# Norms with root and reciprocal on full rows in place of four columns

## The chip, the cores and the metric

The kernel runs on one core of one Trainium2 chip. Its engines are TensorE (PE, matmuls), VectorE (DVE), ScalarE (ACT), GpSimd (POOL) and SyncE (SP, which issues most of the loads). The metric is the device time of one execution in microseconds.

## The reference

Two blocks, one behind the other, on x of 512 positions by 1024 features, all in float32. The first block has four layers (Hyena, window attention, pooling, Hyena), each a mixer and a feed-forward part. The second has one layer (gated delta rule beside latent attention, a merge, and an MLP) with a modulation. Ahead of each of these ten parts stands a norm over the 1024 features:

```python
def rmsnorm(x, g):
    xf = x.astype(jnp.float32)
    y = xf * lax.rsqrt(jnp.mean(xf * xf, axis=-1, keepdims=True) + EPS)
    return (y * g.astype(jnp.float32)).astype(x.dtype)
...
    for i in range(DEPTH):
        h = rmsnorm(x, norm_mix[i])
        ...
        x = x + y
        x = x + swiglu(rmsnorm(x, norm_ffn[i]), ff_w_gate[i], ff_w_up[i], ff_w_down[i])
...
        h = _modulate(_rms(x, norm_attn[l]), mod_x[0], mod_x[1])
        ...
        x = x + mod_x[5] * _sq_relu_mlp(_modulate(_rms(x, norm_mlp[l]), mod_x[3], mod_x[4]), w_mlp_in[l], w_mlp_out[l])
```

## The kernel before

x lies in SBUF as eight tiles of 128 features by 512 positions (`x[:, k, :]`, k from 0 to 7), features on the partitions. A norm sums over features, so over the partitions, and that sum is made by a matmul with ones. `xn` is the buffer for the squares and then for the normed x.

Each engine has its own program, written out by hand stage by stage in the order of `schedule_of`, and the engines wait for each other on semaphores only. Weights come in blocks of 1 MB through a ring of four (`ring`). For the feed-forward parts, the Hyena projections and the MLP each weight and each x is split into a high part of reduced width and the rest: ACT writes the high part (`w_hi`, line 1765; `z_lo` and others, line 1777; of x `x_hi`, line 1772), POOL subtracts it from the weights (`w_lo`, line 779; `ring_r`, line 803), DVE subtracts it from x (`low`, line 2334, into `x_lo` or, in the Hyena layers, `xn_r`). PE then makes three matmuls per tile (lines 904 to 906 for the first block of a stage, 893 to 895 behind it) as soon as the tile's rest is there.

A norm works like this. ACT squares each tile of x when the residual is added (line 1781); DVE adds seven of them into `xn[:, 0]` (`fold`, line 2365). PE multiplies each quarter of 128 positions of that sum, used as the weights, with one column of ones (line 873), then the same for the eighth square (line 877). So the sum for position 128c + p stands on partition p in column c, four columns in all. DVE adds the two groups (lines 2375, 2376), ACT takes the root (line 1810; line 1806 is a root of one number that loads the table of functions early), DVE the reciprocal (line 2380). PE turns the four columns back into a full tile, the same row on all 128 partitions, with the identity (line 882), and DVE multiplies each of the eight tiles of x by the gain and by this tile, which it reads from PSUM (line 2355, in the modulated norms line 2668 with 2669). `rows_read` (line 2386) is a small memset whose semaphore frees the PSUM bank. The banks for such side results are four, taken in turn by a count (`aux`) that every engine keeps in step.

Attention norms its heads with a root and a reciprocal on whole tiles of 128x512 (lines 1105, 1967, 2555, 2557).

Of the kernel before, what the change touches and what calls it, by code (L numbers as in the profile page):

```python
# [268 lines left out]
def run(handlers, schedule):  # L269

    for name, arg in schedule:
        handlers[name](arg)
# [7 lines left out]
def build_program(nc, stream, vecs, tabs, tabs2, x_in, ctx_in, first_mods, scratch, x_keep, diag, solved_t, solved_n, out, schedule):  # L280
# [4 lines left out]
    with ExitStack() as stack:  # L285
# [3 lines left out]
        def sem(name):  # L289
            return stack.enter_context(nc.semaphore(name))  # L290
# [57 lines left out]
        one_col = small_t[:, 7:8]  # L348
        rstd_col = small_t[:, 28:32]

# [17 lines left out]
        def V(name, j=0, n=1, rows=P):  # L368
            at, _ = VEC[name]
            return vec[0:rows, at + j:at + j + n]  # L370
# [25 lines left out]
        folded_set = sem("folded_set")  # L396
        rstd_set = sem("rstd_set")
        root_set = sem("root_set")
# [159 lines left out]
        def _(sp):  # L558
# [43 lines left out]
            def norm(_):  # L602
                n["aux"] += 2
                n["xn"] += DT
# [34 lines left out]
            def modulate(which):  # L639
                n["aux"] += 2 if which else 3  # L640

# [77 lines left out]
        def _(pool):  # L719
# [101 lines left out]
            def passes(aux, acc):  # L821
                def stage(_):
# [4 lines left out]
            nothing = count(0)  # L827
            run({"norm": count(2), "hyena": hyena,
                 "attention": passes(12 + 16 * 5, 88), "pool": passes(0, DT), "ffn": split("ffn", FT + 2 * DT), "mod": nothing,
                 "modulate": lambda which: n.update(aux=n["aux"] + (2 if which else 3)), "decays": count(2),  # L830
                 "gdn": gdn, "mla": nothing, "merge": merge,
# [4 lines left out]
        def _(pe):  # L836
# [31 lines left out]
            def norm(gain):  # L868
                b = open_aux()
                n["fold"] += 1  # L870
                pe.wait_ge(folded_set, n["fold"])
                for c in range(NB):
                    mm(b[:, c:c + 1], xn[:, 0, P * c:P * (c + 1)], ones[:, 0:1], start=True, stop=True)
                n["sq"] += DT
                pe.wait_ge(squares_set, n["sq"])
                for c in range(NB):
                    ins = mm(b[:, NB + c:NB + c + 1], xn[:, DT - 1, P * c:P * (c + 1)], ones[:, 0:1], start=True, stop=True)
                ins.then_inc(aux_full, 1)
                b = open_aux()
                pe.wait_ge(rstd_set, n["fold"])  # L880
                for c in range(NB):
                    ins = mm(b[:, P * c:P * (c + 1)], rstd_col[:, c:c + 1].broadcast_to([P, P]), ident[:], start=True, stop=True)
                ins.then_inc(aux_full, 1)
                n["xn"] += DT
# [842 lines left out]
        def _(act):  # L1727
# [61 lines left out]
            def norm(gain, then=None):  # L1789
# [16 lines left out]
                step(go(small_t[:, 26:27], one_col, ACT.Sqrt))  # L1806
                t = aux.take()
                aux.take()
                act.wait_ge(aux_drained[aux.place(t)], aux.turn(t) + 1)
                signal(go(rstd_col, rstd_col, ACT.Sqrt, bias=eps_col, scale=1.0 / D), root_set)  # L1810
                if split_target(gain) == "hyena":
# [489 lines left out]
        def _(dve):  # L2301
# [40 lines left out]
            def norm(gain):  # L2342
# [3 lines left out]
                if gain == ("norm_mix", 2 * DT):  # L2346
                    nc.vector.memset(sums[:], 0.0)
                    signal(nc.vector.memset(xp[:], 0.0), pads_set)
                    signal(tt_(bs_col, V("pl_b", 0, DT), V("pl_scale", 0, DT), ALU.mult), pads_set)
                t, rows = rstd_rows()  # L2350
                n["xn"] += DT
                target = split_target(gain)
                to = (x_hi_h, xn_r) if target == "hyena" else (x_hi, x_lo)
                for k in range(DT):
                    signal(stt(xn[:, k, :], x[:, k, :], V(gain[0], gain[1] + k), rows, ALU.mult, ALU.mult),  # L2355
                           plain_set if target else xn_set)
                    if target and k:
                        low(k - 1, *to)
                rows_read(t)
                if target:  # L2360
                    low(DT - 1, *to)

            def fold(k):
# [4 lines left out]
                else:  # L2368
                    signal(ins, folded_set)
                    n["sq"] += DT  # L2370

            def rstd_rows():
                t = full(aux, aux_full)
                b = bank(t, True)
                step(nc.vector.tensor_copy(rstd_col, b[:, 0:NB]))
                ins = tt_(rstd_col, b[:, NB:2 * NB], rstd_col, ALU.add)
                drain(ins, t, True)
                n["root"] += 1
                dve.wait_ge(root_set, n["root"])
                signal(nc.vector.reciprocal(rstd_col, rstd_col), rstd_set)  # L2380
                t = full(aux, aux_full)
                return t, bank(t, True)[:]

            def rows_read(t):
                which = aux_drained[t % BANKS]
                nc.vector.memset(small_t[:, 25:26], 0.0).then_inc(which, 1)
                dve.wait_ge(which, t // BANKS + 1)

# [270 lines left out]
            def modulate(which):  # L2659
# [3 lines left out]
                for c in range(2 - which):  # L2663
                    step(ts_(gm[:, c, :], modv[:, scale:scale + DT, c], 1.0, None, ALU.add))
                    step(tt_(gm[:, c, :], gm[:, c, :], gain, ALU.mult))
                t, rows = rstd_rows()
                for k in range(DT):
                    step(stt(xn[:, k, :], x[:, k, :], gm[:, 0, k:k + 1], rows, ALU.mult, ALU.mult))
                    signal(ts_(xn[:, k, :], xn[:, k, :], modv[:, shift + k, 0:1], None, ALU.add), plain_set if which else xn_set)
                    if which and k:  # L2670
                        low(k - 1)
                rows_read(t)
                if which:
# [665 lines left out]
```

## Time and profile before

| | |
|---|---|
| median of 3 timed runs | 4458.51 us (4454.24 to 4459.21) |
| profiled execution | 4452.26 us, span 4450.5 us |
| mean granted clock of PE | 0.956 |
| busy, share of the span | PE 94%, PE weight loads 70%, DVE 47%, POOL 32%, ACT 28% |

The span runs from the first to the last instruction. The granted clock is the share of 2.4 GHz that PE was allowed; its two levels are 2.4 GHz (1.00) and 1.2 GHz (0.50). A matmul in full float32 shows as two records. Where a row of the timeline has a bracket, it gives the engine's idle time before the instruction and what ended it.

### The profile page before, as it was taken

What the parts mean: (1) busy time and instruction counts of PE and PEld (TensorE: products, weight loads), DVE (VectorE), ACT (ScalarE), POOL (GpSimd) and SP (SyncE); (2) the same over time, 40 slices, a digit from 0 to 9 for tenths busy, and PEclk for the clock granted to TensorE, in tenths of its full rate; (3) what the DMA queues carried; (4) which work ended last, traced back from release to release, by engine and by line L of the source; (5) the groups of instructions that cost most, each with busy time, mean ns of one, the idle gap of its engine ahead of it and who ended that gap; (6) DMA issues with size and microseconds to landing.
All of it is one profiled execution on the core that took longest, in us unless ns stands there. A gap on an engine that the chain in (4) does not pass through costs nothing.

```text
span 4450.5 us, 48055 instructions
## 1 busy us (share of the span) xinstructions
PE 4174.7 (94%) x19126; PEld 3110.0 (70%) x19126; DVE 2094.2 (47%) x3123; ACT 1229.7 (28%) x1725; POOL 1442.8 (32%) x834
## 2 busy tenths in 40 slices
PE   7999999999999699999999999989999899998999
PEld 6656788656788478877557887556666665685887
DVE  6567333365323641365773334456664357403322
ACT  3322222135222221233232122322322224422221
POOL 3311344200344144433123442256564000231343
PEclk9999999999999899999999998989999879999999
DMA  6200222210232123221003221121211121221232
GB/s 181 76 15 20 110 108 86 101 55 20 107 107 84 68 101 111 83 81 62 34 29 121 91 104 59 55 59 31 58 33 57 58 76 58 76 95 62 90 104 76
DMA packets 96910, 333.73 MB, mean 75 GB/s; under 512 B 44336, under 2 KB 47536, under 8 KB 67888
## 3 DMA queue, kind: packets, MB, share of 16 engines
q1 hardware_dynamic: 87968, 311.85, 19.8%
q10 hardware_dynamic: 8720, 18.82, 1.7%
q8 instruction: 152, 2.49, 0.2%
q14 instruction: 70, 0.57, 0.0%
HBM read 317.53 MB, written 13.11 MB: 74 GB/s over the span
## 4 chain that ended last, share of the span: by engine, by line
PE 81%; DVE 13%; ACT 2%; POOL 2%; issue 2%; DMA 0%; SPq 0%; DVEq 0%; ACTq 0%; POOLq 0%
PE bank L893 16%; PE bank L894 16%; PE bank L895 16%; PE bank L1328 5%; PE bank L864 5%; PE bank L1095 2%; PE bank L1045 2%; PE bank L1069 1%; PE bank L1308 1%; PE bank L1629 1%; PE bank L1628 1%; PE bank L1650 1%; PE bank L1560 1%; DVE xn L2355 1%; PE bank L1589 1%
## 5 line engine op out<-in xcount | busy, mean ns | idle before, releaser
L779 POOL TENSOR_TENSOR w_lo<-ring,w_hi 128x2048 fp32r<-128x2048 f32 (+2 forms) x200 | 775.1, 3876 | 1519.6 <-ACT w_hi L1765 1519.6
L893 PE MATMUL bank<-x_hi,w_hi 128*128 128x512 f32 x1584 | 618.3, 390 | 9.0 <-POOL w_lo L779 9.0
L895 PE MATMUL bank<-x_hi,w_lo 128*128 128x512 f32 x1584 | 616.9, 389 | 0.0
L894 PE MATMUL bank<-x_lo,w_hi 128*128 128x512 f32 x1584 | 616.7, 389 | 0.0
L1765 ACT ACTIVATE w_hi<-ring 128x2048 fp32r<-128x2048 f32 (+2 forms) x200 | 322.0, 1610 | 867.0 <-PE bank L895 866.0
L893 PE MATMUL bank<-h_hi,w_hi 128*128 128x512 f32 x960 | 373.9, 389 | 0.4
L894 PE MATMUL bank<-h_lo,w_hi 128*128 128x512 f32 x960 | 373.5, 389 | 0.0
L895 PE MATMUL bank<-h_hi,w_lo 128*128 128x512 f32 x960 | 373.4, 389 | 0.0
L893 PEld LDWEIGHTS bank<-x_hi,w_hi 128*128 128x128 f32 x1584 | 297.7, 188 | 72.5 <-POOL w_lo L779 11.1
L895 PEld LDWEIGHTS bank<-x_hi,w_lo 128*128 128x128 f32 x1584 | 297.6, 188 | 62.1
L894 PEld LDWEIGHTS bank<-x_lo,w_hi 128*128 128x128 f32 x1584 | 297.7, 188 | 61.6
L2409 DVE TENSOR_TENSOR xn<-bank,xn 128x512 f32<-128x512 f32 x88 | 60.8, 691 | 587.0 <-PE bank L895 567.6
L1328 PE MATMUL bank<-xn,ring 128*128 128x512 f32 x496 | 237.5, 617 | 1.4 <-DVE work L2712 1.4
L1095 PE MATMUL bank<-work,tab 128*128 128x512 f32 x512 | 225.7, 598 | 12.7 <-ACT work L1908 11.7
L2399 DVE TENSOR_TENSOR x<-bank,x 128x512 f32<-128x512 f32 x72 | 49.8, 691 | 394.1 <-PE bank L895 347.7
L792 POOL TENSOR_TENSOR ring_r<-ring,merge_hi 128x2048 fp32r<-128x2048 f32 x16 | 73.3, 4584 | 499.1 <-ACT merge_hi L2240 499.1
L893 PEld LDWEIGHTS bank<-h_hi,w_hi 128*128 128x128 f32 x960 | 180.2, 188 | 39.5 <-DVE h_lo L2340 2.1
L894 PEld LDWEIGHTS bank<-h_lo,w_hi 128*128 128x128 f32 x960 | 180.2, 188 | 37.3
L895 PEld LDWEIGHTS bank<-h_hi,w_lo 128*128 128x128 f32 x960 | 180.2, 188 | 37.3
L1095 PEld LDWEIGHTS bank<-work,tab 128*128 128x128 f32 x512 | 97.2, 192 | 131.7 <-issue 125.6
L815 POOL TENSOR_TENSOR work<-work,ring 128x1024 f32<-128x1024 f32 x32 | 76.8, 2426 | 265.1 <-ACT work L1877 265.1
L766 POOL TENSOR_TENSOR tab<-tab 56x31 f32<-56x31 f32 (+15 forms) x248 | 152.4, 615 | 19.4
(461 smaller groups left out, 7435.3 us busy)
## 6 DMA issues: line engine op xcount, KB each, us to landing
ring<-stream SPq DMA_DIRECT2D x212, 1024.0 KB, 4.8
ring<-stream SPq DMA_DIRECT2D x64, 704.0 KB, 4.0
ring<-stream SPq DMA_DIRECT2D x36, 512.0 KB, 3.5
xn<-first_mods SPq DMA_DIRECT2D x8, 1024.0 KB, 7.0
ring<-stream SPq DMA_DIRECT2D x4, 1088.0 KB, 5.1
bias_rows<-work ACTq DMA_DIRECT2D x1, 4096.0 KB, 46.2
work<-bias_rows ACTq DMA_DIRECT2D x1, 3072.0 KB, 12.0
tab<-tabs ACTq DMA_DIRECT2D x1, 2624.0 KB, 16.8
```

The source lines that it names most:

```text
L766: solve(tt(W[:, 0:i, i:SUB], W[:, 0:i, i:SUB], part, ALU.subtract))
L779: nc.gpsimd.tensor_tensor(w_lo[:, j % 2, 0:cols], ring[:, k % RING, 0:cols], w_hi[:, j % 2, 0:cols], ALU.subtract).then_inc(wlo_set, 1)
L792: nc.gpsimd.tensor_tensor(ring_r[:, w, 0:2 * DT * P], ring[:, w, 0:2 * DT * P], merge_whi[j % 2][:], ALU.subtract).then_inc(wlo_set, 1)
L815: nc.gpsimd.tensor_tensor(pair, pair, decay[:, pq:pq + 1, :].broadcast_to([P, 2, 512]), ALU.mult).then_inc(filt_set, 1)
L864: ins = mm(b[:], w[:, at + k, :], rhs[k] if isinstance(rhs, list) else rhs[:, k, :], start=(k == 0), stop=(k == kt - 1))
L893: mm(b[:], hi[:, at + k, :], rhs_hi, start=(k == 0), stop=False)
L894: mm(b[:], hi[:, at + k, :], rhs_lo[:, k, :], start=False, stop=False)
L895: ins = mm(b[:], lo[:, at + k, :], rhs_hi, start=False, stop=(k == kt - 1))
L1045: ins = mm(b[:, 256 * p:256 * (p + 1)], U[:, 4 * ft + 2 * kind + p, ct * P:(ct + 1) * P], inv[kind][:, p, ft, :], start=(j == 0), stop=(j ...
L1095: ins = mm(b[:], fwd[kind][:, p, q, ft * P:(ft + 1) * P], source(kind)[:, 2 * p + q, :], start=(q == 0), stop=(q == 1))
L1328: ins = mm(b[:, 0:TC] if ctx else b[:], w[:, at + k, :], src[:, k, :], start=(k == 0), stop=(k == DT - 1))
L1765: signal(go(w_hi[:, j % 2, 0:cols], ring[:, k % RING, 0:cols], ACT.Copy), whi_set)
```

## The change

In all ten norms the sums are made as full rows: two matmuls with the whole matrix of ones as weights and the squares as the moving side, added up in one bank. Every partition then holds the sum of every position. ACT takes the root of this 128x512 tile into SBUF (`rstd`), DVE the reciprocal of 128x512 in place, which also frees the bank, and the multiplications read `rstd` from SBUF instead of a bank. The four columns, the two small DVE operations, PE's second visit and the closing memset are gone, and each norm takes one side bank instead of two. The norm of the context, the pool layer and the order of stages are untouched.

```diff
             def norm(gain):            # PE
                 b = open_aux()
                 n["fold"] += 1
                 pe.wait_ge(folded_set, n["fold"])
-                for c in range(NB):
-                    mm(b[:, c:c + 1], xn[:, 0, P * c:P * (c + 1)], ones[:, 0:1], start=True, stop=True)
+                mm(b[:], ones[:], xn[:, 0, :], start=True, stop=False)
                 n["sq"] += DT
                 pe.wait_ge(squares_set, n["sq"])
-                for c in range(NB):
-                    ins = mm(b[:, NB + c:NB + c + 1], xn[:, DT - 1, P * c:P * (c + 1)], ones[:, 0:1], start=True, stop=True)
-                ins.then_inc(aux_full, 1)
-                b = open_aux()
-                pe.wait_ge(rstd_set, n["fold"])
-                for c in range(NB):
-                    ins = mm(b[:, P * c:P * (c + 1)], rstd_col[:, c:c + 1].broadcast_to([P, P]), ident[:], start=True, stop=True)
-                ins.then_inc(aux_full, 1)
+                mm(b[:], ones[:], xn[:, DT - 1, :], start=False, stop=True).then_inc(aux_full, 1)
                 n["xn"] += DT
...
                 step(go(small_t[:, 26:27], one_col, ACT.Sqrt))      # ACT
-                t = aux.take()
-                aux.take()
-                act.wait_ge(aux_drained[aux.place(t)], aux.turn(t) + 1)
-                signal(go(rstd_col, rstd_col, ACT.Sqrt, bias=eps_col, scale=1.0 / D), root_set)
+                t = full(aux, aux_full)
+                signal(go(rstd, bank(t, aux=True)[:], ACT.Sqrt, bias=eps_col, scale=1.0 / D), root_set)
...
-                t, rows = rstd_rows()                               # DVE
+                t = aux.take()
+                n["root"] += 1
+                dve.wait_ge(root_set, n["root"])
+                drain(nc.vector.reciprocal(rstd, rstd), t, True)
...
                 for k in range(DT):
-                    signal(stt(xn[:, k, :], x[:, k, :], V(gain[0], gain[1] + k), rows, ALU.mult, ALU.mult),
+                    signal(stt(xn[:, k, :], x[:, k, :], V(gain[0], gain[1] + k), rstd, ALU.mult, ALU.mult),
                            plain_set if target else xn_set)
                     if target and k:
                         low(k - 1, *to)
-                rows_read(t)
...
-            def rstd_rows():
-                t = full(aux, aux_full)
-                b = bank(t, True)
-                step(nc.vector.tensor_copy(rstd_col, b[:, 0:NB]))
-                ins = tt_(rstd_col, b[:, NB:2 * NB], rstd_col, ALU.add)
-                drain(ins, t, True)
-                n["root"] += 1
-                dve.wait_ge(root_set, n["root"])
-                signal(nc.vector.reciprocal(rstd_col, rstd_col), rstd_set)
-                t = full(aux, aux_full)
-                return t, bank(t, True)[:]
```

`modulate` on DVE changes in the same way as `norm`.

What stands on VectorE from the last addition of squares in the first norm, before (`bank` is PSUM, `vec` the gains, `small_t` holds the four columns):

```order
L2365 TENSOR_TENSOR xn<-xn 128x512 [waits squares_set,vec_step] x5
L2375 COPY small_t<-bank 128x4 [waits aux_full,folded_set]
L2376 TENSOR_TENSOR small_t<-bank,small_t 128x4 [waits vec_step]
L2380 RECIPROCAL small_t<-small_t 128x4 [waits root_set,aux_drained0]
L2355 SCALAR_TENSOR_TENSOR xn<-x,vec,bank 128x512 [waits aux_full,rstd_set]
L2355 SCALAR_TENSOR_TENSOR xn<-x,vec,bank 128x512 [waits plain_set]
L2334 TENSOR_TENSOR xn_r<-xn,x_hi_h 128x512 [waits xhi_set,plain_set]
```

and at the same place of the changed kernel (its line numbers are its own; `rstd_t` holds `rstd`):

```order
L2355 TENSOR_TENSOR xn<-xn 128x512 [waits squares_set,vec_step] x5
L2341 RECIPROCAL rstd_t<-rstd_t 128x512 [waits root_set,folded_set]
L2346 SCALAR_TENSOR_TENSOR xn<-x,vec,rstd_t 128x512 [waits aux_drained0]
L2346 SCALAR_TENSOR_TENSOR xn<-x,vec,rstd_t 128x512 [waits plain_set]
L2322 TENSOR_TENSOR xn_r<-xn,x_hi_h 128x512 [waits xhi_set,plain_set]
```

The copy and the addition are gone, the reciprocal has full rows, and the multiplications have three SBUF operands and no wait for PE.

On TensorE the same place before, with the first matmuls of the Hyena layer behind it:

```order
L873 MATMUL bank<-ones,xn 128x1 [waits folded_set,consts_set]
L873 MATMUL bank<-ones,xn 128x1 x3
L877 MATMUL bank<-ones,xn 128x1 [waits squares_set]
L877 MATMUL bank<-ones,xn 128x1 x3
L882 MATMUL bank<-ident,small_t 128x128 [waits rstd_set]
L882 MATMUL bank<-ident,small_t 128x128 x3
L1720 MATMUL bank<-tab,vec 16x512 [waits tab_landed,vec_landed]
L952 MATMUL bank<-tab,vec 64x512
L904 MATMUL bank<-x_hi_h,z_lo 128x512 [waits xn_set,wlo_set]
```

and in the changed kernel:

```order
L870 MATMUL bank<-xn,ones 128x512 [waits folded_set,consts_set]
L873 MATMUL bank<-xn,ones 128x512 [waits squares_set]
L1710 MATMUL bank<-tab,vec 16x512 [waits tab_landed,vec_landed]
L942 MATMUL bank<-tab,vec 64x512
L894 MATMUL bank<-x_hi_h,z_lo 128x512 [waits xn_set,wlo_set]
```

Twelve small matmuls have become two long ones, and PE's wait for the reciprocal in the middle is gone; it waits for the normed x alone.

## Rows read from the trace of the kernel before

**Rows 1.** The page: chain that ended last, shares of the span by engine

```profile
PE 81%; DVE 13%; ACT 2%; POOL 2%; issue 2%; DMA 0%; SPq 0%; DVEq 0%; ACTq 0%; POOLq 0%
```

**Rows 2.** Timeline at 471.7: start us, us, engine line op [idle before]

```profile
471.05 0.69 DVE L2365 TENSOR_TENSOR xn<-xn 128x512 f32<-128x512 f32 x1
...
471.89 1.02 PE L873 MATMUL bank<-ones,xn 128*128 128x1 f32 x8 [1.73 <-DVE xn L2365]
...
477.25 1.53 DVE L2355 SCALAR_TENSOR_TENSOR xn<-x,vec,bank 128x512 f32<-128x512 f32 x2 [2.30 <-PE bank L882]
...
479.66 0.76 PE L904 MATMUL bank<-x_hi,w_hi 128*128 128x512 f32 x1 [2.52 <-DVE x_lo L2334]
```

**Rows 3.** Lines of DVE, 400 to 4450: busy us, mean ns | idle before

```profile
L2355 DVE SCALAR_TENSOR_TENSOR xn<-x,vec,bank 128x512 f32<-128x512 f32 x56 | 41.9, 748 | 17.6 <-PE bank L882 15.9
...
L2668 DVE SCALAR_TENSOR_TENSOR xn<-x,gm,bank 128x512 f32<-128x512 f32 x16 | 12.0, 747 | 5.1 <-PE bank L882 4.6
...
L2380 DVE RECIPROCAL small_t<-small_t 128x4 f32<-128x4 f32 x9 | 1.6, 178 | 4.7 <-ACT small_t L1810 4.7
...
L2375 DVE COPY small_t<-bank 128x4 f32<-128x4 f32 x9 | 1.5, 161 | 18.4 <-PE bank L877 18.4
...
L2376 DVE TENSOR_TENSOR small_t<-bank,small_t 128x4 f32<-128x4 f32 x9 | 1.5, 161 | 0.3
...
L2347 DVE MEMSET work<- 128x1056 f32 x1 | 0.9, 938 | 0.3 <-DVE xn L2365 0.3
...
L2665 DVE TENSOR_TENSOR gm<-gm,vec 128x8 f32<-128x8 f32 x3 | 0.5, 168 | 0.1
```

**Rows 4.** Timeline of one root and reciprocal in attention

```profile
872.32 1.02 PE L1105 MATMUL bank<-work,tab 128*128 128x512 f32 x2
...
873.44 0.69 ACT L1967 ACTIVATE work<-bank,small_t 128x512 f32<-128x512 f32 x1 [0.26 <-PE bank L1105]
...
874.23 3.35 DVE L2555 RECIPROCAL work<-work 128x512 f32<-128x512 f32 x1 [17.41 <-ACT work L1967]
...
877.69 0.75 DVE L2557 SCALAR_TENSOR_TENSOR work<-bank,vec,work 128x512 f32<-128x512 f32 x1
```

**Rows 5.** Timeline: matmuls at half clock, in three norms

```profile
15.91 1.84 PE L873 MATMUL bank<-ones,xn 128*128 128x1 f32 x8 [15.91 <-DVE xn L2365]
...
22.64 1.89 PE L1720 MATMUL bank<-tab,vec 33*16 33x512 f32 x2
...
1932.08 1.83 PE L873 MATMUL bank<-ones,xn 128*128 128x1 f32 x8 [2.02 <-DVE xn L2365]
...
2750.90 1.54 PE L877 MATMUL bank<-ones,xn 128*128 128x1 f32 x8
```

**Rows 6.** Timeline: DVE beside POOL in the first norm and behind it

```profile
22.33 4.51 POOL L803 TENSOR_TENSOR ring_r<-ring,z_lo 128x2048 fp32r<-128x2048 f32 x1 [20.71 <-ACT z_lo L1777]
...
22.82 1.53 DVE L2355 SCALAR_TENSOR_TENSOR xn<-x,vec,bank 128x512 f32<-128x512 f32 x2 [2.23 <-PE bank L882]
...
24.39 2.99 DVE L2334 TENSOR_TENSOR xn_r<-xn,x_hi_h 128x512 fp32r<-128x512 f32 x1
...
41.31 4.49 POOL L803 TENSOR_TENSOR ring_r<-ring,z_lo 128x2048 fp32r<-128x2048 f32 x1 [14.48 <-ACT z_lo L1777]
...
42.15 3.94 DVE L2432 TENSOR_SCALAR work<-work 64x512 f32<-64x512 f32 x1 [4.60 <-ACT work L1854]
...
62.07 0.75 DVE L2451 SCALAR_TENSOR_TENSOR work<-work,vec 128x512 f32<-128x512 f32 x1
...
62.44 4.86 POOL L803 TENSOR_TENSOR ring_r<-ring,z_lo 128x2048 fp32r<-128x2048 f32 x1 [4.47 <-ACT z_lo L1777]
...
62.86 5.00 DVE L2452 SCALAR_TENSOR_TENSOR work<-work,vec 128x512 f32<-128x512 f32 x1
```

**Rows 7.** Stretch (us, five engines' busy, granted clock); timeline at 1558

```profile
477.00:484.00 7.00, 4.48 (x11) 3.46 (x11) 6.47 (x9) 3.12 (x5) 0.00 (x0) 0.50 0.01 2
...
1558.45 4.50 POOL L779 TENSOR_TENSOR w_lo<-ring,w_hi 128x2048 fp32r<-128x2048 f32 x1 [69.80 <-ACT w_hi L1765]
```

More of the change, by code:

```diff
@@ L348, in build_program @@
         one_col = small_t[:, 7:8]
-        rstd_col = small_t[:, 28:32]
         def carve(*sizes):
@@ L396, in build_program @@
         folded_set = sem("folded_set")
-        rstd_set = sem("rstd_set")
         root_set = sem("root_set")
@@ L602, in norm @@
             def norm(_):
-                n["aux"] += 2
+                n["aux"] += 1
                 n["xn"] += DT
@@ L639, in modulate @@
             def modulate(which):
-                n["aux"] += 2 if which else 3
+                n["aux"] += 1 if which else 2
             def decays(_):
@@ L827, in _ @@
             nothing = count(0)
-            run({"norm": count(2), "hyena": hyena,
+            run({"norm": count(1), "hyena": hyena,
                  "attention": passes(12 + 16 * 5, 88), "pool": passes(0, DT), "ffn": split("ffn", FT + 2 * DT), "mod": nothing,
-                 "modulate": lambda which: n.update(aux=n["aux"] + (2 if which else 3)), "decays": count(2),
+                 "modulate": lambda which: n.update(aux=n["aux"] + (1 if which else 2)), "decays": count(2),
                  "gdn": gdn, "mla": nothing, "merge": merge,
@@ L2370, in fold @@
                     n["sq"] += DT
-            def rstd_rows():
-                t = full(aux, aux_full)
-                b = bank(t, True)
-                step(nc.vector.tensor_copy(rstd_col, b[:, 0:NB]))
-                ins = tt_(rstd_col, b[:, NB:2 * NB], rstd_col, ALU.add)
-                drain(ins, t, True)
-                n["root"] += 1
-                dve.wait_ge(root_set, n["root"])
-                signal(nc.vector.reciprocal(rstd_col, rstd_col), rstd_set)
-                t = full(aux, aux_full)
-                return t, bank(t, True)[:]
[L2384 to L2387, printed above, removed]
             def residual(bias_name=None, scale_name=None, fold_squares=True):
@@ L2665, in modulate @@
                     step(tt_(gm[:, c, :], gm[:, c, :], gain, ALU.mult))
-                t, rows = rstd_rows()
+                t = aux.take()
+                n["root"] += 1
+                dve.wait_ge(root_set, n["root"])
+                drain(nc.vector.reciprocal(rstd, rstd), t, True)
                 for k in range(DT):
-                    step(stt(xn[:, k, :], x[:, k, :], gm[:, 0, k:k + 1], rows, ALU.mult, ALU.mult))
+                    step(stt(xn[:, k, :], x[:, k, :], gm[:, 0, k:k + 1], rstd, ALU.mult, ALU.mult))
                     signal(ts_(xn[:, k, :], xn[:, k, :], modv[:, shift + k, 0:1], None, ALU.add), plain_set if which else xn_set)
@@ L2671, in modulate @@
                         low(k - 1)
-                rows_read(t)
                 if which:
```

## The prediction

> **What bounds the kernel now.** I read the chain that ended last first: it is 81% on TensorE (PE) [rows 1]. So only time in which PE waits, or in which something that it waits for is late, can change the end. Then I read the timeline around the norms. A norm is a place where everything waits for one chain. In [rows 2] the last partial sum of squares on VectorE (DVE) ends at 471.74 (471.05 + 0.69). PE then makes eight small matmuls (16 records), DVE and ScalarE (ACT) work on four columns, PE spreads them over the rows again, and the first multiplication of x starts at 477.25. This chain from the fold to the first multiplication took 5.51 us. PE's first real product starts at 479.66, 2.41 us behind the multiplication. PE has no other work in that time, so the length of this chain is paid in full, once per norm. There are ten such norms.
>
> DVE's groups of lines give the same chain for the nine norms behind the first [rows 3]: idle before L2375 18.4, its busy 1.5; L2376 1.5 and 0.3; idle before L2380 4.7, its busy 1.6; waits for PE before L2355 and L2668 15.9 and 4.6. That is 48.5 us. In the pool layer's norm two memsets stand in this chain (2 x 0.94 and 0.5 of idle time), and in the two norms with modulation small work on the gains adds 1.2 (L2665 0.5 and 0.1, L2664 the same). Together 52.1 us, or 5.8 per norm.
>
> **What replaces it.** Per norm: two matmuls 128x512 with a matrix of ones, a square root 128x512 on ACT straight from PSUM, a reciprocal 128x512 on DVE, and the same eight multiplications, now with the factor from SBUF. Attention of this very kernel has the same three steps in the same shapes [rows 4], so nothing has to be guessed but what surrounds them:
> - fold to PE: 0.15 (471.74 to 471.89, [rows 2]);
> - two matmuls. One is two records, which take 1.02 together and 0.59 alone, so 0.43 lies between starts [rows 4]. Four records: 1.02 + 2 x 0.43 = 1.88;
> - PE to ACT 0.10, root 0.69, ACT to DVE 0.10 [rows 4];
> - reciprocal 3.35, then 0.11 until the next instruction [rows 4].
>
> The sum is 6.38 us. The reciprocal on four columns took 0.18 [rows 3]: the price of the change is that this one instruction becomes 3.2 us longer, and what it buys is the second visit to PE (2.30 of wait in [rows 2]), the two small DVE operations and the shorter sum on four columns. Nine norms: 9 x 6.38 = 57.4 against 52.1, **+5.3 us**. The two memsets of the pool norm are hidden in this sum, because DVE now waits for ACT anyway.
>
> The eight multiplications keep their price: 748 ns with the factor from PSUM [rows 3], and 0.75 for the same instruction with all tensors in SBUF (L2451 at 62.07 [rows 6]). The memset of L2386 that frees the bank goes. At 59 ns it stood mostly under a rounding on ACT; only in the pool norm is DVE itself the pace, -0.14 with its gap.
>
> **TensorE's clock in the sums.** PE has had no work for 1.73 us when the sums begin (the idle time in the row of L873, [rows 2]), and the granted clock falls from 2.4 to 1.2 GHz somewhere in the gap. In the norm of 1932 the half clock had come before the sums: the same eight records took 1.83 instead of 1.02 [rows 5, 2]. The new sums are longer, so more of them meet it. At half clock two records of 512 columns take 1.89 (L1720 [rows 5]), so four take 1.89 + 2 x 0.86 = 3.61, that is +1.73 over 1.88. If the clock falls where it fell before: +1.73 in the norm of 1932; about +1.0 in the norm of 2750, where the second group of eight records took 1.54 [rows 5]; and, as my estimate, +0.5 each in the norms near 845 and 1500, where it fell later. Bounds: nothing, and 9 x 1.73 = 15.6. I take the same places: **+3.7 us**. After the chain PE restarts at half clock now as before (0.50 granted from 477 to 484, [rows 7]); the phase of that is left out as even on the mean, with about 1 us either way per norm and some 2 us over all.
>
> **VectorE and GpSimd.** In the first norm GpSimd (POOL) subtracts the high part of the weights from 22.33 to 26.84 while DVE multiplies [rows 6]. The two multiplications with a PSUM factor ran through it undisturbed (1.53 for two). The first subtraction with two SBUF tiles, L2334, did not: it took 2.99 instead of 0.69 and ended at 27.38, 0.54 after POOL. The multiplication form that will be used now, all from SBUF, shows the same: L2452 at 62.86 took 5.00 and ended 0.56 after POOL's subtraction that ended at 67.30 [rows 6]. So in the first norm: the sums start at 15.91 at half clock (the small group took 1.84, [rows 5]) and end at 15.91 + 3.61 = 19.5, about where the small ones do; root and reciprocal end at 23.8; then the first multiplication is held until 27.40. The second takes 0.78 with its gap, the subtraction 0.7: it ends at 28.9 instead of 27.38, **+1.5 us**. If the multiplication were not held, it would be 0. This delay is passed on: the last tile releases ACT's rounding, behind that stands the rounding of the next weights, and for that POOL waited 14.48 us at 41.31 [rows 6], with PE behind it. In the norm of 1556 POOL works from 1558.45 to 1562.95 [rows 7]; by my sum the reciprocal ends at 1562.8, so the first multiplication meets only its last 0.1 us. In the other eight norms POOL has ended its work before DVE multiplies, or starts after it.
>
> The reciprocal itself reads one SBUF tile. The trace has no long reciprocal beside POOL. The nearest row is L2432, a one-tile operation that was held from 42.15 until 0.29 after POOL's end [rows 6]; another one-tile row is L2355, which was not held. Held, the reciprocal at 1559.4 would end near 1566.2 (+3.4), and the one at 20.4, if it held POOL in its turn until 23.8, would move POOL's end by 1.5. I take it as not held: it takes 3.35 us for 512 elements where a multiplication takes 0.75 [rows 4], so it is the slowest reader of its tile of them all and has no use for a second way into SBUF, and in this it is nearer to L2355 than to the quick L2432, whose 64x512 would be done in well under a us. The Trainium skill says this as a rule (SBUF — State Buffer, Who interferes with whom): a VectorE instruction with at most one SBUF input that is outside the 2-port modes does not contend with GpSimd, one with two SBUF inputs contends with a GpSimd instruction that reads SBUF. By it the first price is 0 and the multiplication's is 1.5; for the reciprocal no row here shows it.
>
> **Sum.** +5.3 + 3.7 - 0.1 + 1.5 = **+10.4 us**. The profiled execution took 4452.26 us (span 4450.5), the median of the timed runs is 4458.51, 6.25 above it; I carry that difference over: 4458.5 + 10.4 = 4468.9, say 4469, 0.23% more. A measurement of this kernel tells about 0.2% (8.9 us) from no change, so the forecast stands just over that bound.
>
> **Rivals.**
> - *The clock spares the sums.* If the full clock holds for the 1.9 us of sums in all nine norms, 3.7 falls away: +6.7, 4465. And the norm of 1932 is cheaper than before. For it: in [rows 2] the group ran at full clock, 1.02. Against: the new sums are longer, and the row of 1932 had lost the clock before they began. Chance 0.2.
> - *The reciprocal is caught by POOL.* +10.4 + 3.4 + 1.5 = +15.3, 4474. For it L2432's row, against it the rate. Chance 0.1.
> - *Not slower: the dense sums keep PE's clock up.* Before, the 16 records in the gap were 128x1 and did little; now PE multiplies 1.9 us in full. If the clock then stayed at 2.4 GHz until the restart, the 3.7 would go, and in the four norms in which PE itself sets the pace behind the restart (471, 845, 1127 and 2377) so would the half-clock stretch, (484 - 479.7) / 2 = 2.2 each at least [rows 2, 7], 8.6 in all. 10.4 - 3.7 - 8.6 = -1.9, 4457. It decides from the point where at least five of these things happen. Against it: PE stands still for 4.4 us behind the sums and another 2.4 until the first product, longer in one piece than the gap in the middle of the chain before, in which the clock was low. The Trainium skill gives a rule that bears on this (TensorE: Matmul & The Clock Gate, Why this matters for your kernels): avoid idle gaps between bursts of matmuls, or the clock goes back to half. By this rule the rival doesn't come about, and the trace agrees as far as it goes: half clock from 477 to 484 behind a gap of this length [rows 7]. Chance 0.06.
> - *The steps overlap more than I think*, with a result within 5 us of before: nothing in the timeline stands beside the chain that could do it. Chance 0.04.
>
> **How the numbers follow.** The forecast has 0.6, with its own range of +7.5 to +13.5 (what share of the clock's 15.6 is met, and the restart). Within it some 0.45 of 0.6 lie above 8.9 us. Slower: 0.45 + 0.1 = 0.55. Within 0.2%: 0.15 + 0.2 + 0.05 + 0.03 = 0.42 with rounding. Faster: 0.03. The range for 8 of 10 reaches from the first rival's lower side to the second rival with some us of a run's own spread: 4461 to 4477.
>
> **What would show it.** Right: ten reciprocals of 128x512 at 3.35 us; about 6.4 us from fold to first multiplication where the clock is full and up to 8.1 where it isn't; no L882; in the first norm a multiplication of over 3 us that ends 0.56 after POOL; PE's busy time lower, which buys nothing. Wrong: multiplications of 0.75 beside POOL; PE records of 0.39 right after the gap; a reciprocal of over 3.4 us; a chain under 6 us anywhere.

## The result and the profile after

The changed kernel takes 4472.98 us (median of 7 runs, 4467.73 to 4479.67), the kernel before 4458.51 in the same comparison (7 runs, 4453.41 to 4461.94): ratio 1.0032, 95% interval 1.002 to 1.0044, so 14.5 us slower. The profiled execution took 4467.73, the shortest of the seven (span 4465.9, before 4450.5: +15.4).

The page after, busy time by engine, the granted clock in its 40 slices, and the chain that ended last:

```profile
PE 4158.9 (93%) x18926; PEld 3081.6 (69%) x18926; DVE 2120.0 (47%) x3093; ACT 1233.6 (28%) x1725; POOL 1442.7 (32%) x834
...
PEclk9999999999999899999989999989998879999999
...
PE 81%; DVE 13%; ACT 2%; POOL 2%; issue 1%; DMA 0%; SPq 0%; DVEq 0%; ACTq 0%; POOLq 0%
```

The page tells little: 200 PE records fewer, 26 us more on DVE, and shares of the chain as before [rows 1]. The timeline after, of the norm of [rows 2]:

```profile
466.62 0.69 DVE L2355 TENSOR_TENSOR xn<-xn 128x512 f32<-128x512 f32 x1
...
467.46 1.10 PE L870 MATMUL bank<-xn,ones 128*128 128x512 f32 x2 [1.73 <-DVE xn L2355]
468.39 1.02 PE L873 MATMUL bank<-xn,ones 128*128 128x512 f32 x2
...
469.51 0.69 ACT L1798 ACTIVATE rstd_t<-bank,small_t 128x512 f32<-128x512 f32 x1 [0.69 <-PE bank L873]
470.30 3.35 DVE L2341 RECIPROCAL rstd_t<-rstd_t 128x512 f32<-128x512 f32 x1 [2.99 <-ACT rstd_t L1798]
473.69 1.54 DVE L2346 SCALAR_TENSOR_TENSOR xn<-x,vec,rstd_t 128x512 f32<-128x512 f32 x2
```

From the fold's end (467.31) to the first multiplication it is 6.38 us. It is 6.38 in eight of the nine later norms, the modulated ones too, and 6.67 in the one near 2386. The groups of lines after, DVE and PE from 400 to 4450 (busy us, mean ns | idle before), stand where [rows 3] stood:

```profile
L2346 DVE SCALAR_TENSOR_TENSOR xn<-x,vec,rstd_t 128x512 f32<-128x512 f32 x56 | 42.1, 752 | 2.0
...
L2341 DVE RECIPROCAL rstd_t<-rstd_t 128x512 f32<-128x512 f32 x7 | 23.5, 3354 | 18.7 <-ACT rstd_t L1798 18.7
...
L2642 DVE RECIPROCAL rstd_t<-rstd_t 128x512 f32<-128x512 f32 x2 | 6.7, 3353 | 4.8 <-ACT rstd_t L1798 4.8
```

```profile
L870 PE MATMUL bank<-xn,ones 128*128 128x512 f32 x18 | 9.9, 630 | 15.3 <-DVE xn L2355 15.3
L873 PE MATMUL bank<-xn,ones 128*128 128x512 f32 x18 | 9.2, 592 | 0.0
```

The sums ran at 2.4 GHz in all nine norms: each of the 18 records of L873 took 592 or 593 ns, and of L870 the first of each norm took 667 and the second 592 (at half clock, in the first norm, they took 1061 and more). The 6.67 near 2386 does not come from PE: there the sums ended at 2388.59 and ACT began its root at 2388.97, 0.38 behind them, where it is 0.10 in the norm above; why is open. The timeline after, of the first norm:

```profile
20.52 3.35 DVE L2341 RECIPROCAL rstd_t<-rstd_t 128x512 f32<-128x512 f32 x1 [4.78 <-ACT rstd_t L1798]
...
22.44 4.50 POOL L801 TENSOR_TENSOR ring_r<-ring,z_lo 128x2048 fp32r<-128x2048 f32 x1 [20.82 <-ACT z_lo L1767]
23.91 4.36 DVE L2346 SCALAR_TENSOR_TENSOR xn<-x,vec,rstd_t 128x512 f32<-128x512 f32 x2
...
28.31 0.69 DVE L2322 TENSOR_TENSOR xn_r<-xn,x_hi_h 128x512 fp32r<-128x512 f32 x1
...
29.15 0.77 PE L894 MATMUL bank<-x_hi_h,z_lo 128*128 128x512 f32 x1 [7.16 <-DVE xn_r L2322]
```

The reciprocal kept its 3.35 with POOL beside it for the last 1.4 us. Near 1556 a whole reciprocal (from 1556.32) lay inside a subtraction of POOL (1555.34 to 1559.84) and took 3.35 too. Two multiplications took 4.36 in place of 1.53, and PE's first product came at 29.15, 1.6 later than before (27.53).

**Where the time went.** I cut both profiled executions at the end of each norm's fold (the last addition of squares) and at its last multiplication, and compare the pieces (us). A stage is what lies between a norm's last multiplication and the next fold's end.

| piece | before | after | difference |
|---|---|---|---|
| ten chains, fold to first multiplication | 59.3 | 65.9 | +6.6 |
| eight multiplications, ten times | 102.4 | 103.3 | +0.8 |
| first Hyena stage | 436.0 | 430.0 | -6.1 |
| second Hyena stage | 427.3 | 439.9 | +12.6 |
| delta-rule and latent stage | 1303.3 | 1306.1 | +2.8 |
| all other stages and the end | 2122.2 | 2120.9 | -1.3 |

The chains and multiplications give 7.4, half of what was measured. The other half lies in stages whose instructions were not changed. A half-clock stretch is from here on one in which PE was granted 1.2 GHz. In the Hyena stages one iteration of the loop over filters takes 61.5 us or 65.0 us. Two stretches of one iteration's length, us, five engines' busy time and the granted clock; before:

```profile
2155.00:2216.50 61.50, 56.08 (x194) 34.00 (x193) 40.84 (x52) 16.74 (x25) 9.30 (x4) 0.97 0.00 1
```

and after, then three pieces of such an iteration:

```profile
2155.00:2220.00 65.00, 59.56 (x194) 35.66 (x193) 40.98 (x52) 16.74 (x25) 9.34 (x4) 0.92 0.00 1
...
2222.00:2228.00 6.00, 6.00 (x16) 2.88 (x16) 5.76 (x9) 2.16 (x4) 0.00 (x0) 1.00 0.00 1
2228.70:2232.10 3.40, 3.40 (x28) 2.94 (x26) 1.29 (x2) 0.00 (x0) 0.00 (x0) 1.00 0.00 0
2232.20:2239.00 6.80, 6.80 (x14) 3.70 (x15) 0.18 (x1) 1.22 (x3) 0.97 (x1) 0.50 0.00 0
```

The same 194 matmul records, 3.5 us more of PE busy. Both iterations have one half-clock stretch of 3.4 us behind PE's wait for the spectra's product; the long one has a second, of 6.8 us. Ahead of that second stretch PE was busy without a gap, but with 28 records in 3.4 us: these are the filter-magnitude sums, sixteen matmuls against a single column of ones. The stretch begins at 2232.22, 2.9 us after the sums did and inside them. The lines on PE after (L1075 is the sums, L1059 the filter's taps behind them):

```profile
2222.48 7.03 PE L1085 MATMUL bank<-work,tab 128*128 128x512 f32 x16
2229.35 4.20 PE L1075 MATMUL bank<-ones,work 128*128 128x1 f32 x32
2233.41 9.91 PE L1059 MATMUL bank<-ring,work 128*128 128x512 f32 x16
```

Before, the same sixteen were followed by taps at full clock, 7.12 in place of 9.91:

```profile
2227.25 3.63 PE L1085 MATMUL bank<-ones,work 128*128 128x1 f32 x32
2230.74 7.12 PE L1069 MATMUL bank<-ring,work 128*128 128x512 f32 x16
```

In every profile of a kernel with these sums a stage that has had one long iteration has only long ones from there on. So a stage comes out at 427 to 431 with none and at 436 to 442 with one to four. That a small change of timing decides between the two was then my theory 1; theory 2 was that a delay costs its own length and the change has a further price of its own.

### The profile page after: what moved, and what is told of

Its sections match the earlier page's. It is cut to its first block, busy times and chain, and to the rows that moved or that the text cites. A ratio compares the mean times of both kernels' runs of the same rounds, so it can differ in the third digit from the quotient of the medians.

```text
span 4465.9 us, 47595 instructions
## 1 busy us (share of the span) xinstructions
PE 4158.9 (93%) x18926; PEld 3081.6 (69%) x18926; DVE 2120.0 (47%) x3093; ACT 1233.6 (28%) x1725; POOL 1442.7 (32%) x834
## 4 chain that ended last, share of the span: by engine, by line
PE 81%; DVE 13%; ACT 2%; POOL 2%; issue 1%; DMA 0%; SPq 0%; DVEq 0%; ACTq 0%; POOLq 0%
PE bank L883 16%; PE bank L884 16%; PE bank L885 16%; PE bank L1318 5%; PE bank L862 5%; PE bank L1085 2%; PE bank L1035 2%; PE bank L1059 1%; PE bank L1298 1%; PE bank L1619 1%; PE bank L1618 1%; PE bank L1640 1%; DVE xn L2346 1%; PE bank L1550 1%; PE bank L1579 1%
## 5 line engine op out<-in xcount | busy, mean ns | idle before, releaser
L1085 PE MATMUL bank<-work,tab 128*128 128x512 f32 x512 | 225.9, 599 | 12.8 <-ACT work L1896 11.7
```

What stands on the lines that cost most here:

```text
L1085: ins = mm(b[:], fwd[kind][:, p, q, ft * P:(ft + 1) * P], source(kind)[:, 2 * p + q, :], start=(q == 0), stop=(q == 1))
```

## Experiments

All ratios are to the kernel before, timed on the same chip in the same series; each series had another chip. In the first four series its median was 4456.4, 4455.3, 4455.7 and 4454.1 (4442.9 to 4465.3 over all); in the fifth, with a_wide64_again alone, it was 4464.0. Stage lengths are from each run's one profiled execution.

**b_head1**: a delay at the start alone, in the kernel before.

```diff
-                    for k in range(1, DT - 1):
+                    for k in range(1, DT - 2):
                         fold(k)
+                    step(nc.vector.memset(kbuf2[:, 0:772], 0.0))
+                    step(nc.vector.memset(kbuf2[:, 0:96], 0.0))
+                    fold(DT - 2)
```

> The kernel before with two memsets on DVE (772 and 96 columns, some 0.9 us together) ahead of the last partial sum of the first norm, nothing else changed. Everything behind it starts 0.9 us later. Theory 1 (the part of the slowdown that the norm chains don't explain comes from half-clock stretches in the Hyena and delta-rule stages, and their number depends on the moment at which a stage begins): the total moves by something else than 0.9 us, anywhere from -8 to +10 us, and the two Hyena stages (436.0 and 427.3 us in the profile before, from the first norm multiplication... to the next fold) change length by steps of about 1.7 us, the time that a half-clock stretch of 3.4 us costs. Theory 2 (a delay costs its own length, and the change has a further price of its own): +0.9 us, both stages as before within 1 us.

Measured: 4473.52 (10 runs, 4465.13 to 4480.36), ratio 1.0038 [1.0026, 1.0051]. A delay of 0.9 us costs 17. That is outside theory 1's own range (-8 to +10) as well as far from theory 2's 0.9. Both Hyena stages were long, 439.3 and 440.1. The timed runs say the same as the profile: five took 4465.1 to 4470.3 at a mean granted clock of 0.952 to 0.953, the other five 4476.8 to 4480.4 at 0.950, and the kernel before in the same series runs from 0.958 in its shortest run (4443.1) to 0.953 in its longest (4464.2).

**b_head2**: the two memsets twice, 1.8 us.

> As the run before it, with twice the memsets (some 1.8 us). Theory 1: the total moves by another amount than with 0.9 us and not by twice as much, with stage lengths in steps of 1.7 us. Theory 2: +1.8 us.

Measured: 4475.59 (6 runs), ratio 1.0045 [1.0028, 1.0061]; Hyena stages 431.0 and 441.3. The second 0.9 us costs 2.1, which is less than the spread of the six runs (4467.20 to 4481.19): not 17 again.

**b_slow**: the kernel before with the same two memsets ahead of the reciprocal in each of the ten norms.

```diff
+                for cols in (772, 96):
+                    step(nc.vector.memset(kbuf2[:, 0:cols], 0.0))
                 signal(nc.vector.reciprocal(rstd_col, rstd_col), rstd_set)
```

> The kernel before with the same two memsets (0.9 us) in each of the ten norm chains, ahead of the reciprocal on four columns, so that each chain is 0.9 us longer as in the changed kernel (0.87), with the sums, the PSUM factor and all else as before. Theory 1 (chain length and its shifts are all there is): +9 us of chains, and of the stretches anything from -8 to +10, so that the total can equal the changed kernel's +14.5. Theory 2 (the change has a further price beside its chains): +9 us and no more, both Hyena stages as before.

Measured: 4467.62 (12 runs), ratio 1.0025 [1.0014, 1.0036]. Its chains sum to 71.0, 11.7 more than before, and it costs 11.2: ten delays cost less than one at the head, and in its profiled execution (4463.39; the runs reach 4475.03) both Hyena stages were short (431.2, 429.9). So the excess does not grow with the delay. This run alone would also fit theory 2, which had +9.

**a_psum**: the changed kernel with the reciprocal written to the norm's PSUM bank and read from there.

```diff
-                drain(nc.vector.reciprocal(rstd, rstd), t, True)
+                rows = bank(t, True)[:]
+                step(nc.vector.reciprocal(rows, rstd))
...
-                    signal(stt(xn[:, k, :], x[:, k, :], V(gain[0], gain[1] + k), rstd, ALU.mult, ALU.mult),
+                    signal(stt(xn[:, k, :], x[:, k, :], V(gain[0], gain[1] + k), rows, ALU.mult, ALU.mult),
```

> The changed kernel, with the reciprocal written to its PSUM bank and the eight multiplications reading it there, and the closing memset back. If GpSimd's hold on the multiplication with SBUF operands cost 1.6 us in the first norm, then the first multiplication there takes 0.75 us and not 3.6, the first product of the matmul engine comes 1.5 us sooner than in the changed kernel (27.6 and not 29.15), and the other chains stay at 6.4 us. If the hold is not the cause, the first product stays at 29.1. The total: -1.5 us against the changed kernel, beside what the stretches do.

Measured: 4473.62 (8 runs), ratio 1.0033 [1.002, 1.0046], as the changed kernel. The first norm's timeline shows that its own purpose was reached:

```profile
22.40 4.51 POOL L801 TENSOR_TENSOR ring_r<-ring,z_lo 128x2048 fp32r<-128x2048 f32 x1 [20.78 <-ACT z_lo L1767]
23.88 1.53 DVE L2347 SCALAR_TENSOR_TENSOR xn<-x,vec,bank 128x512 f32<-128x512 f32 x2
...
25.45 2.01 DVE L2322 TENSOR_TENSOR xn_r<-xn,x_hi_h 128x512 fp32r<-128x512 f32 x1
...
27.61 0.77 PE L894 MATMUL bank<-x_hi_h,z_lo 128*128 128x512 f32 x1 [6.03 <-DVE xn_r L2322]
```

The multiplications run free again, the next operation with two SBUF operands (L2322, 2.01 for 0.69) is the one held, and PE starts at 27.61 instead of 29.15. The 1.5 us are real, and lost again: both Hyena stages were long (442.1, 440.1).

**b_wide64, a_wide64, b_wide128**: take away the suspected trigger. The filter-magnitude sums get 64 (128) columns of ones in place of one; the same edit in the kernel before (b) and the changed one (a).

```diff
-                        ins = mm(b[:, ct:ct + 1], mags[:, pq, ct * P:(ct + 1) * P], ones[:, 0:1],
+                        ins = mm(b[:, 64 * ct:64 * (ct + 1)], mags[:, pq, ct * P:(ct + 1) * P], ones[:, 0:64],
...
-                    drain(nc.vector.reciprocal(invn[:, 4 * c:4 * c + 4], bank(t, True)[:, 0:4]), t, True)
+                    drain(nc.vector.reciprocal(invn[:, 4 * c:4 * c + 4], bank(t, True)[:, 0:256:64]), t, True)
```

> The kernel before, with the sixteen N=1 matmuls of each filter-magnitude sum in the Hyena stages (L1085, moving operand 128x1) given a moving operand of 64 columns of ones instead; results and their readers are the same, so only the columns that TensorE streams change. Theory 1 (recurring half-clock stretches of the Hyena stages are the cause of the 8 us that the norm chains do not explain, and the 6.8 us stretch of each loop iteration is set off by these N=1 matmuls): the 6.8 us stretches are gone from both Hyena stages, each stage lasts 427 to 432 us in every run, and the kernel's times gather at 4443 to 4452, 5 to 10 below its median of 4456, with less spread than the 21 us of before. Theory 2 (the stages' length has another cause, and the clock only follows it): both lengths, 427 to 431 and 436 to 442, still occur, the times still spread over some 20 us, and the median moves by under 3 us. If the 64 columns cost time by themselves (at most 16 x 0.1 us in eight places), up to 13 us come on top.

> The changed kernel with the same edit (64 columns in place of one in the filter-magnitude matmuls of the Hyena stages). Theory 1: its Hyena stages also last 427 to 432 us, and its distance to the kernel before with the same edit is what the ten chains cost, 5.5 + 1.6 = +7 us, not +14.5: about 4450 to 4459. Theory 2: the distance between the two stays at 14 to 15 us.

> The kernel before with 128 columns in place of one in the same sixteen matmuls. Theory 1: as with 64 columns, no 6.8 us half-clock stretch, times within 4 us of those with 64 columns plus what 64 more columns cost (16 x 0.1 us in eight places at most, if the weight loads do not hide them: up to 13 us). Theory 2: no change of the spread.

Measured:

| kernel | median us, runs | lowest, highest | ratio [95%] | Hyena stages |
|---|---|---|---|---|
| b_wide64 | 4447.29, 11 | 4440.41, 4449.66 | 0.9977 [0.9968, 0.9986] | 428.7, 427.4 |
| a_wide64 | 4455.10, 11 | 4453.39, 4459.10 | 1.0 [0.9991, 1.0009] | 428.8, 425.5 |
| b_wide128 | 4446.31, 11 | 4439.61, 4449.01 | 0.9974 [0.9965, 0.9983] | 427.9, 425.9 |

Theory 1 holds, but for two stages a little shorter than its 427 to 432 (425.5, 425.9) and some runs under its 4443. All six stages are short and hold no second half-clock stretch in the loop over filters, and the distance between changed and before falls from 14.5 to 7.8. The count over all profiles is sharper: in the seven kernels with one column the clock fell 2.2 to 5.0 us after the start of 37 of the 56 sums; in the seven with 64 or 128 columns it fell within 12 us behind none of 56. Where it fell in the first 2.9 us, inside the sums, it stayed low for 6.8 or 10.2 us (22 cases); later, for 3.4 (13) or 6.8 (2). In the timeline of b_wide64 the sums are followed by taps at full clock:

```profile
2220.42 3.68 PE L1085 MATMUL bank<-ones,work 128*128 128x64 f32 x32
2223.93 7.09 PE L1069 MATMUL bank<-ring,work 128*128 128x512 f32 x16
```

and the 63 more columns cost next to nothing: the groups of this line on PE, kernel before, then 64, then 128 columns,

```profile
L1085 PE MATMUL bank<-ones,work 128*128 128x1 f32 x256 | 29.6, 250 | 0.0
```

```profile
L1085 PE MATMUL bank<-ones,work 128*128 128x64 f32 x256 | 29.4, 273 | 0.0
```

```profile
L1085 PE MATMUL bank<-ones,work 128*128 128x128 f32 x256 | 29.9, 275 | 0.0
```

29.6 us in all against 29.4 and 29.9. The first of these has half-clock pieces in it; at full clock one sum took 3.63, 3.68 and 3.73 us, so the price is 0.4 or 0.8 us in all eight. The Trainium skill (Perfetto Trace Analysis, Matmul Optimizations) says that the matmul engine scales power by utilization and that matmuls should go back to back in batches. The trace adds to it: these did go back to back, 3.40 us busy of 3.40, and the clock still fell in them or behind them in 37 of 56 cases with one column each, and in none of 56 with 64 or 128.

**b_tail**: the 0.9 us of b_head1 in the last norm alone.

```diff
+                n["norms"] = n.get("norms", 0) + 1
+                if n["norms"] == 10:
+                    for cols in (772, 96):
+                        step(nc.vector.memset(kbuf2[:, 0:cols], 0.0))
                 signal(nc.vector.reciprocal(rstd_col, rstd_col), rstd_set)
```

> The kernel before with the same 0.9 us of memsets as at its head in the earlier run, but in the last norm alone, behind both Hyena stages and the delta-rule stage. Theory 1 (a delay costs more than itself only where it moves the Hyena stages against the clock's stretches): +1 us to the kernel before, same distribution (4443 to 4465). Theory 2 (a shift at any place costs this much, or the memsets themselves do, or the excess belongs to another stage): +10 to +17 us as at the head.

Measured: 4453.91 (11 runs), ratio 0.9997 [0.9988, 1.0006]. A delay behind the Hyena stages costs nothing that can be measured.

**b_head1_wide64**: both edits in the kernel before.

> The kernel before with the 0.9 us of memsets at its head (which alone cost 17 us) and the 64 columns of the filter-magnitude matmuls together. Theory 1 (the head delay costs more than itself only because it makes the Hyena stages fall more often into the pattern with the 6.8 us half-clock stretch): the excess is gone, the time is that of the 64-column kernel, 4447.3, plus 1 to 2, so 4447 to 4450, and both Hyena stages last 425 to 430 us. Theory 2 (the head delay acts through something else, and the 64 columns gain by themselves): both effects add, 4447 + 17 = 4464.

Measured: 4447.39 (11 runs, 4445.88 to 4451.54), ratio 0.9984 [0.9975, 0.9993]; Hyena stages 427.9 and 427.6. That is 0.1 above b_wide64 by the medians and, since the two were timed in different series, 3 by the ratios (0.9977). The delay that cost 17 us costs 0 to 3 once the magnitude sums have 64 columns. Theory 2 had 4464.

**a_psum_wide64**: the changed kernel with both edits.

> The changed kernel with the 64 columns (4455.1, spread 6 us) and with the reciprocal written to the norm's PSUM bank, from which the multiplications read it, so that the first multiplication is not an SBUF-SBUF one beside GpSimd. In the changed kernel the held first multiplication put TensorE's first product at 29.15; with PSUM rows alone it was at 27.61. Theory (the hold is worth the 1.5 us of the prediction): 4455.1 - 1.5 = about 4453.6. Rival (the start is not on the path that sets the end, or the PSUM rows cost as much in the ten norms): 4455 or more.

Measured: 4447.29 (11 runs, 4444.66 to 4450.12), ratio 0.9983 [0.9974, 0.9992]; 7.8 below a_wide64, not 1.5 (by the ratios of the two series 7.6). Both expectations missed. Between the profiled executions 1.5 of the 10.4 lie in the first norm's multiplications (11.90 for 13.44), 2.8 in the first Hyena stage (426.0), and 7.2 in the delta-rule stage: 1302.6 for 1309.8.

**a_wide64_again**: is that the execution or the kernel?

> A second profiled execution of the changed kernel with the 64 columns, to see what belongs to the kernel and what to the execution. In the first its delta-rule stage lasted 1309.8 us, against 1302.6 with PSUM rows, and that was 7 of the 10 us between those two profiled executions. If a kernel falls into one pattern of half-clock stretches whatever its start, the stage lasts 1309 to 1310 again and the Hyena stages 425 to 429. If the pattern is drawn anew in each execution, the stage lasts anything from 1302 to 1310.

Measured: 4455.94 (8 runs, 4453.82 to 4458.40), ratio 0.9984 [0.9973, 0.9996]; the kernel itself repeats within 0.8 us on another chip, while the kernel before moved by 8.6, so a ratio of one series does not compare with that of another to better than 0.0016. The delta-rule stage lasted 1309.8 again, the Hyena stages 428.9 and 425.5. One stretch in that stage, in the first execution and in the second:

```profile
3400.00:3800.00 400.00, 378.25 (x1823) 250.21 (x1821) 197.70 (x488) 121.06 (x270) 17.09 (x31) 0.86 0.19 66
```

```profile
3400.00:3800.00 400.00, 378.24 (x1823) 250.47 (x1822) 197.68 (x489) 121.06 (x270) 17.42 (x31) 0.86 0.19 66
```

So in that stage two executions on two chips fall into the same half-clock stretches, and the 7.2 us between this kernel and a_psum_wide64 look like the kernels' own. It is not so for every kernel: the eleven runs of b_wide64 fall into two groups, four at 4440.4 to 4441.7 and seven at 4446.6 to 4449.7, and only one of the latter was profiled. Which instruction of that stage decides was not tried.

**b_acc_wide64**: a version to beat both. The kernel before with 64 columns, the eighth square accumulated into the same four columns, and the root taken from PSUM.

```diff
-                for c in range(NB):
-                    mm(b[:, c:c + 1], xn[:, 0, P * c:P * (c + 1)], ones[:, 0:1], start=True, stop=True)
...
-                    ins = mm(b[:, NB + c:NB + c + 1], xn[:, DT - 1, P * c:P * (c + 1)], ones[:, 0:1], start=True, stop=True)
+                    mm(b[:, c:c + 1], xn[:, 0, P * c:P * (c + 1)], ones[:, 0:1], start=True, stop=False)
+                    ins = mm(b[:, c:c + 1], xn[:, DT - 1, P * c:P * (c + 1)], ones[:, 0:1], start=False, stop=True)
...
-                signal(go(rstd_col, rstd_col, ACT.Sqrt, bias=eps_col, scale=1.0 / D), root_set)
+                signal(go(rstd_col, bank(t, aux=True)[:, 0:NB], ACT.Sqrt, bias=eps_col, scale=1.0 / D), root_set)
...
-                step(nc.vector.tensor_copy(rstd_col, b[:, 0:NB]))
-                ins = tt_(rstd_col, b[:, NB:2 * NB], rstd_col, ALU.add)
-                drain(ins, t, True)
```

> The kernel before with the 64 columns, and with a shorter norm chain: the eighth square is accumulated into the same four PSUM columns as the seven folded ones, ScalarE takes the root from them directly, and VectorE's copy and addition of four columns are gone. From the rows of the kernel before, the copy and the addition with their handovers take some 0.45 us of each chain: ten chains of about 5.0 to 5.1 us in place of 5.5, and 4447.3 - 4.5 = 4443. If sums that cannot begin before the eighth square add as much as the copy saves: 4447. If clock stretches shift again: 4440 to 4455.

Measured: 4440.26 (5 runs, 4431.43 to 4443.31), ratio 0.996 [0.9947, 0.9973], the fastest here. Its ten chains sum to 52.8 against 57.3 in b_wide64, the 4.5 expected. The other 2.5 of its 7.0 us are less than the spread of its runs. The profiled execution was its shortest, with Hyena stages of 425.9 and 425.9 and a delta-rule stage of 1302.6.

## Why the prediction was right, and where not

The predicted 4469 stands against 4473, inside the range, and slower as forecast. But the sum was right partly by luck: one term was too large and a larger one was missing.

- **Chain, +5.3.** Measured 57.7 against 52.2 in the nine later norms, +5.5. The pieces from attention's rows gave 6.38, and 6.38 it was in eight of the nine; the ninth has 0.3 more ahead of ACT's root. Right.
- **The clock in the sums, +3.7.** Measured 0: all 36 records of the nine norms were at full clock. Mis-sized: the step "If the clock falls where it fell before" took its place in the time line as fixed. Before, it fell 0.1 to 3.6 us behind the fold's end in the nine norms; after, 4.6 to 11.4 us, always behind the sums, which end 2.1 us behind the fold's end. In the norm shown it fell at 474.4, and in the norm near 1930 at 1935.3, where before it had fallen at 1932.1, in the sums. So the first rival (the clock spares the sums) is what the chains did. That the denser sums moved the fall is likely but was not tried by itself.
- **First norm, +1.5.** Measured +1.6 at PE's first product, and a_psum took it away (27.61). The reciprocal was not held, as taken, though POOL worked beside it from 22.44 in the first norm and through all of it near 1556; the second rival falls. By the rule of the Trainium skill cited in the prediction (SBUF — State Buffer, Who interferes with whom) the hold goes with the second SBUF operand, and the trace agrees: it moved from L2346 to L2322 when the factor went to PSUM.
- **Memsets of the pool norm, -0.1.** Too small to be told.
- **Multiplications, 0.** Measured +0.3 in the nine later norms: with the factor from SBUF eight take 0.03 us more (752 for 748 ns each).
- **Not slower, by a clock that holds.** A part of it occurred: the half-clock stretch behind the norm shown was 6.8 us (from 474.4) where it had been 10.2, and the stages other than Hyena and delta rule together gained 2.3 (the end behind the last norm lost 1.1). It did not reach the point that decides.
- **Missing.** "The phase of that is left out as even on the mean ... some 2 us over all." This step failed. The experiments put 14.5 - 7.8 = 6.7 us of the result on the Hyena stages' second half-clock stretch, which has to do with the norm only through the time at which the loop is entered. The 6.7 is rough, since the interval of the 14.5 is 9 to 20 us; the two profiled executions have 6.5 between them in these stages. The remaining 7.8 is near what the terms make: 5.5 for the chains, 1.6 for the first norm and 0.3 for the multiplications, 7.4. That they meet so well is luck in part: between the profiled executions of a_wide64 and b_wide64 chains and multiplications differ by 9.4 us (b_wide64's chains took 57.3, not 59.3), and all the rest gives 3.2 of it back. And a_psum_wide64 warns that the delta-rule stage can hide several us of either sign: with PSUM rows the full-row norm is as fast as four columns (4447.29 both; ratios 0.9983 and 0.9977).

So the forecast of +10.4 came near 14.5 with 3.7 us for something that did not happen and nothing for the 6.7 that did.

What stays open: why entering the loop earlier or later by under 1 us selects the long iterations, and why the kernel before falls into either kind from run to run. The profiled executions are too few to tie this to a clock phase, and the one profile of a kernel does not give its share of long stages.

## What to carry to other kernels

Sum the chain on the path from rows of the same shapes; that part was exact to 0.2 us. Then look for recurring half-clock stretches in loops elsewhere: where a kernel has them, a change of 1 us can cost 17 or nothing, and a difference of a few tenths of a per cent says little about the edit until they are gone. A run of matmuls with one column each is a cheap suspect: here 63 or 127 more columns cost 0.05 or 0.1 us per sixteen matmuls.

## What the runs showed of the hardware

- TensorE fell to 1.2 GHz in or behind sixteen 128x1 float32 matmuls that kept it busy without a gap (3.40 of 3.40 us), 2.2 to 5.0 us after their start and for 3.4 to 10.2 us, in 37 of the 56 such sums profiled; with 64 or 128 columns in none of 56. The spread of times was 16 to 21 us in the kernel before in its first four series (15 to 33 runs each), 12 in b_tail (11 runs), and 5 to 9 in the six sets of 8 to 11 runs with 64 or 128 columns (12 in the five runs of b_acc_wide64).
- Sixteen float32 matmuls with 128x128 weight loads took 3.63, 3.68 and 3.73 us with 1, 64 and 128 columns at full clock.
- A 128x512 reciprocal on VectorE takes 3.35 us, from SBUF to SBUF (3.35) or to PSUM (3.36), and GpSimd's 4.5 us subtraction beside it changes nothing.
- A VectorE multiplication or subtraction with two SBUF tiles beside that subtraction is held until 0.5 to 0.6 us behind its end (3.58 us in place of 0.75, 2.01 in place of 0.69); with one of them in PSUM the multiplication is not (1.53 for two).
- The pattern of the granted clock can repeat: two executions of a_wide64, on two chips, had the same 1309.8 us stage with the same share of clock. b_wide64's runs fell into two groups 5 us apart.
